# One change to a three-block decoder kernel on one core: the order in which late halves are consumed at six block joints, the start, one table load, and the end of a differential attention

## The reference

```
h    = rms_norm(x, g)                       # mean of squares over the row, then a power of -0.5
y    = swiglu(h, w_in, w_out)               # feed-forward: keys f00, f01, f10, f11 (and f3)
x    = x + rms_norm(y, g2) * factor
gate = sigmoid(x_normed @ w_ple_gate)       # keys p0, p1: one projection times one gate
...
# differential attention (key df), 8 heads, two score maps per head
D    = softmax(q1 k1) - lambda * softmax(q2 k2)
o    = rms_norm(D @ v) per head;  x = x + rms_norm(o @ diff_w_out)
```

## Time and profile before

| | |
|---|---|
| median of three runs | 2924.79 us |
| profiled execution | 2925.86 us |
| its span, first to last instruction | 2924.1 us |
| PE busy | 2855.8 us, 98% |
| DVE busy | 1951.1 us, 67% |
| ACT busy | 1633.9 us, 56% |
| mean granted clock of PE | 0.993 |

### The profile page before, as it was taken

How to read it: one execution, slowest core, us unless ns; L and a number is a source line. 1 busy time by engine, 2 the same in 40 slices (tenths; PEclk the granted TensorE clock), 3 DMA queues, 4 the chain that set the end, 5 groups by cost and what they waited for, 6 DMA issues and landing times.

```text
span 2924.1 us, 44449 instructions
## 1 busy us (share of the span) xinstructions
PE 2855.8 (98%) x17894; PEld 2554.0 (87%) x17894; DVE 1951.1 (67%) x3360; ACT 1633.9 (56%) x2792; POOL 341.2 (12%) x309
## 2 busy tenths in 40 slices
PE   7999999899989999999999999999999999999999
PEld 6878888788878877799998999999888889989997
DVE  5656765676566656758874898777555566656775
ACT  5544654665546555456655444777545455655664
POOL 0000000000010001000000444896000000000000
PEclk9999999999999999999999999999999999999999
DMA  6644556356434554445445554434555564536454
GB/s 205 198 165 145 174 193 224 118 185 217 162 113 144 201 194 147 144 127 169 122 145 187 177 184 159 144 131 145 198 191 193 195 234 133 161 87 208 146 185 154
DMA packets 304525, 490.33 MB, mean 168 GB/s; under 512 B 10865, under 2 KB 236529, under 8 KB 295617
## 3 DMA queue, kind: packets, MB, share of 16 engines
q1 hardware_dynamic: 303184, 480.09, 49.6%
q0 software_dynamic: 1136, 7.41, 0.7%
HBM read 485.36 MB, written 2.10 MB: 167 GB/s over the span
## 4 chain that ended last, share of the span: by engine, by line
PE 88%; DVE 6%; ACT 3%; DMA 1%; issue 1%; POOL 0%; SPq 0%; DVEq 0%; POOLq 0%; ACTq 0%
PE ps L608 30%; PE ps L538 11%; PE ps L542 11%; PE ps L539 10%; PE ps L687 10%; PE ps L686 5%; PE ps L1123 2%; DVE halves L1367 2%; PE ps L559 1%; DVE XX L1405 1%; PE ps L1158 1%; ACT XX L2588 1%; ACT AR L2611 1%; PE ps L1178 1%; PE ps L491 1%
## 5 line engine op out<-in xcount | busy, mean ns | idle before, releaser
L2563 ACT ACTIVATE halves<-raw 128x1024 fp32r<-128x1024 f32 (+1 forms) x842 | 878.4, 1052 | 704.3 <-PE ps L608 336.3
L1367 DVE TENSOR_TENSOR halves<-raw,halves 128x1024 fp32r<-128x1024 f32 (+1 forms) x806 | 965.2, 1219 | 224.3 <-ACT halves L2563 221.6
L538 PE MATMUL ps<-XX,halves 128*128 128x256 f32 (+1 forms) x2360 | 586.4, 286 | 0.0
L539 PE MATMUL ps<-XX,halves 128*128 128x256 f32 (+1 forms) x2360 | 578.2, 283 | 0.0
L608 PE MATMUL ps<-halves,XX 128*128 128x512 f32 x2256 | 527.3, 394 | 5.4 <-DVE XX L1405 2.7
L608 PEld LDWEIGHTS ps<-halves,XX 128*128 128x128 f32 x2256 | 425.9, 190 | 100.9 <-issue 7.9
L538 PEld LDWEIGHTS ps<-XX,halves 128*128 128x128 f32 (+1 forms) x2360 | 451.4, 191 | 2.6 <-issue 2.0
L539 PEld LDWEIGHTS ps<-XX,halves 128*128 128x128 f32 (+1 forms) x2360 | 451.9, 191 | 0.2
L542 PE MATMUL ps<-XX,halves 128*128 128x256 f32 (+1 forms) x2360 | 331.5, 283 | 0.7 <-DVE halves L1367 0.7
L608 PE MATMUL ps<-halves,R 128*128 128x512 f32 x1404 | 322.1, 390 | 0.0
L687 PE MATMUL ps<-XX,halves 128*128 128x512 f32 x1264 | 318.5, 393 | 2.2 <-DVE XX L1405 2.2
(11 more groups left out here) (368 smaller groups left out, 3518.4 us busy)
## 6 DMA issues: line engine op xcount, KB each, us to landing
raw<-in_w_ffn_in SPq DMA_DIRECT2D x88, 1024.0 KB, 5.1
raw<-in_w_in SPq DMA_DIRECT2D x74, 1024.0 KB, 5.3
raw<-in_uT SPq DMA_DIRECT2D x64, 1024.0 KB, 4.8
raw<-in_peer_v SPq DMA_DIRECT2D x64, 1024.0 KB, 4.9
raw<-in_w_ffn_out SPq DMA_DIRECT2D x44, 1024.0 KB, 4.8
raw<-in_w_up SPq DMA_DIRECT2D x24, 1024.0 KB, 5.7
raw<-in_mlstm_w_in SPq DMA_DIRECT2D x12, 1024.0 KB, 5.4
raw<-in_w_down SPq DMA_DIRECT2D x12, 1024.0 KB, 4.9
```

What stands on the lines that cost most here:

```text
L538: mm(o[:, ts], hi[:, q, 0:M], xh[:, k0 + q, ts], start=first and q == 0, stop=False)
L539: mm(o[:, ts], hi[:, q, 0:M], xl[:, k0 + q, ts], start=False, stop=False)
L1367: te.tensor_tensor(lo, src, hi.bitcast(F32), ALU.subtract).then_inc(k.lo_made, 1)
L2563: act(hi, src, ACT.Copy).then_inc(k.hi_made, 1)
```

## The change

It has five edits.

1. In `four`, the term with the low weights comes second and the term with the low half of x last. In DVE's `residual`, at joints that lead to `four`, the low halves of the next weights come first, then the sum into x of side 1, and `enter(0)` is split: four tiles ahead of `x_moment(1)`, four behind it (after p0, four tiles ahead of the sum and four behind it).
2. The start: x is loaded first, in two transfers, and the constants after it. Squares, moment and power are marked per side.
3. In `both_out`, a sigmoid of one column is issued at the end of f01 and f11, after the first two copies.
4. In ml, `decays` starts two steps (one weight piece) later on all three engines.
5. In df, DVE does mix of head 7 before out_pair(2), and ACT and DVE make no halves by `weights()` at t = 0 to 2 but by hand: up to t = 2 first, then t = 3 and t = 4 (ACT after out_pair(2), DVE after attention(8)); the rest comes after out_pair(6).

```diff
@@ tensor_engine, four
             for q in range(3):
-                if q == 2:
+                if q == 1:
                     for m in range(n, n + 4):
                         pe.wait_ge(*k.lo_of(m))
...
-                    for need in ready(t, j, q == 0):
+                    for need in ready(t, j, q < 2):
...
-                             act[q == 1][:, t, j * 128:(j + 1) * 128],
-                             k.halves[:, 0:4, q // 2, t * 128:(t + 1) * 128], ...
+                             act[q == 2][:, t, j * 128:(j + 1) * 128],
+                             k.halves[:, 0:4, q % 2, t * 128:(t + 1) * 128], ...
@@ mlstm decays: PE and ACT range(4) -> range(6), DVE range(2) -> range(4)
@@ sync_engine
+    for j in range(2):
+        load(k.x[:, j], d["x"].rearrange("b (j p) n -> p (b j) n", p=128)[:, j]).then_inc(*dma[f"x_in{j}"].mark(j))
     load(k.cols[:], d["cpack"])...
     load(k.ident[:], ...); load(k.iota[:], ...); load(k.ar(0, 256), ...)
-    load(k.x, d["x"].rearrange("b (j p) n -> p (b j) n", p=128)).then_inc(*dma["x_in"].mark("x"))
@@ vector_engine, residual
         x_moment(0)
+        tokens_next = key in ("f01", "f11", "p1")
+        if not banks:
+            low_to(k.next_four(key) - 3)
+        x_low(0)
+        if not banks:
+            pre(1)
+            if tokens_next:
+                enter(0)
+            low_to(k.next_four(key))
+        if row:
+            weighted(1, 1)
             weighted(1, 0)
             ...
             variance(1)
         if banks:
-            enter(0)
+            if tokens_next:
+                enter(0)
             low_to(k.next_four(key) if more else -1)
+        if row and not banks and not tokens_next:
+            enter(0, range(4))
         if row:
             summed(1)
         else:
             added(1)
+        if not tokens_next:
+            if banks:
+                enter(0, range(4))
+            else:
+                enter(0, range(4, 8))
         x_moment(1)
+        if banks and not tokens_next:
+            enter(0, range(4, 8))
         x_low(1)
         enter(1)
@@ vector_engine, down
-            weights()
+            if t < hold:
+                v.cur += 1
+            else:
+                weights()
@@ vector_engine, diff
+            if t == 0:
+                low_to(v.cur + 2)
+                out_pair(0)
+                for _ in attention(6):
+                    pass
+                last = attention(8)
+                next(last)
+                out_pair(2)
+                for _ in last:
+                    pass
+                low_to(v.cur + 4)
+            if t == 3:
+                for _ in attention(10):
+                    pass
+                out_pair(4)
+                out_pair(6)
-        down("df", 8, True, 1.0, each=before)
+        down("df", 8, True, 1.0, each=before, hold=3)
@@ scalar_engine, diff (down has hold too)
+            if t == 0:
+                high_to(a.cur + 2)
+                out_pair(0)
+                for _ in attention(6):
+                    pass
+                out_pair(2)
+                high_to(a.cur + 4)
+                for _ in attention(8):
+                    pass
@@ scalar_engine
     def both_out(l, c):
         for j in range(2):
             ple_out(l, c, j)
+        if c == 0:
+            act(k.st[:, 90:91], k.cols[:, 0:1], ACT.Sigmoid)
```

More of the change, by code:

```diff
@@ L139, in later, with nothing @@
     yield from side
-def nothing(_):
+def nothing(*_):
     pass
@@ L745, in decays @@
         def decays():
-            for _ in range(4):
+            for _ in range(6):
                 yield
@@ L1282, in normed @@
             gp.wait_ge(*s["xn_high"].need((prev, j)))
-    inverse_root(st[:, 28:30], st[:, 26:28], s["x_var"].need("in"), "in")
+    for j in range(2):
+        inverse_root(st[:, 28 + j:29 + j], st[:, 26 + j:27 + j], s["x_var"].need(("in", j)), ("in", j))
     residual("f00", True, True)
@@ L1397, in turned_x, with of @@
         hi, lo = dst
-        def of(j):
+        def of(j, tiles=range(8)):
             ts = slice(j * 128, (j + 1) * 128)
-            for c in range(8):
+            for c in tiles:
                 c0 = c - c % per
@@ L1521, in tokens, with down @@
                 evac(s0, j)
-    def down(key, KT, row, factor, more=True, each=None):
+    def down(key, KT, row, factor, more=True, each=None, hold=0):
         for t in range(KT):
@@ L1645, in decays @@
             yield from gates()
-            for _ in range(2):
+            for _ in range(4):
                 yield
@@ L2499, in vector_engine @@
     te.tensor_copy(k.mask[:, 0:128], mst[:, 128:256]).then_inc(*step.mark("constants"))
-    v.wait_ge(*s["x_square"].need("in"))
-    chained(te.tensor_reduce(st[:, 26:28], st[:, 16:20].rearrange("p (j h) -> p j h", h=2), AX.X, ALU.add))
-    te.tensor_scalar(st[:, 26:28], st[:, 26:28], 1.0 / 1024, 1e-6, ALU.mult, ALU.add) \
-        .then_inc(*s["x_var"].mark("in"))
-    v.wait_ge(*s["pow"].need("in"))
-    for j in range(2):
+    for j in range(2):
+        v.wait_ge(*s["x_square"].need(("in", j)))
+        chained(te.tensor_tensor(st[:, 26 + j:27 + j], st[:, 16 + 2 * j:17 + 2 * j], st[:, 17 + 2 * j:18 + 2 * j], ALU.add))
+        te.tensor_scalar(st[:, 26 + j:27 + j], st[:, 26 + j:27 + j], 1.0 / 1024, 1e-6, ALU.mult, ALU.add) \
+            .then_inc(*s["x_var"].mark(("in", j)))
+    for j in range(2):
+        v.wait_ge(*s["pow"].need(("in", j)))
         te.tensor_scalar(XN[:, j, 512:1024], x[:, j, 512:1024], st[:, 28 + j:29 + j], None, ALU.mult) \
@@ L2672, in tokens, with down @@
                 evac(s0, j)
-    def down(key, KT, row, factor, more=True, each=None, mid=nothing):
+    def down(key, KT, row, factor, more=True, each=None, mid=nothing, hold=0):
         for t in range(KT):
@@ L2677, in down @@
                 each(t)
-            weights()
+            if t < hold:
+                a.cur += 1
+            else:
+                weights()
         residual(key, lambda j, h: ps[:, aux.of((key, "o", 2 * j + h)), :], True, row, factor, more,
@@ L2927, in before @@
         def before(t):
-            for i in {0: (6, 8), 3: (10,)}.get(t, ()):
-                if i < 10:
-                    out_pair(i - 6)
-                for _ in attention(i):
-                    pass
-                if i == 10:
-                    out_pair(4)
-                    out_pair(6)
-        down("df", 8, True, 1.0, each=before)
+            if t == 0:
+                high_to(a.cur + 2)
+                out_pair(0)
+                for _ in attention(6):
+                    pass
+                out_pair(2)
+                high_to(a.cur + 4)
+                for _ in attention(8):
+                    pass
+            if t == 3:
+                for _ in attention(10):
+                    pass
+                out_pair(4)
+                out_pair(6)
+        down("df", 8, True, 1.0, each=before, hold=3)
     def attend(key, src, E_, yT, release):
@@ L3322, in ffn3 @@
         down("f3", 24, True, 1.0, more=False)
-    a.wait_ge(*k.dma["x_in"].need("x"))
     for j in range(2):
+        a.wait_ge(*k.dma[f"x_in{j}"].need(j))
         for h in range(2):
```

23 lines of the change are left out of this document (4 added, 19 removed).

## The result

| | before | after |
|---|---|---|
| median | 2925.63 us | 2910.24 us |
| its runs | 2924.44 to 2928.08 | 2905.11 to 2911.18 |
| span of the profiled execution | 2924.1 us | 2908.7 us |
| PE busy | 2855.8 us | 2856.3 us |
| mean granted clock | 0.993 | 0.994 |

The ratio is 0.9944, with an interval of 0.9928 to 0.9959: 15.4 us less, where 19.6 were predicted. The four launches of the kernel after lie 6 us apart, and the fastest of them has the highest mean granted clock (0.996; the others 0.993 to 0.995). So the forecast of 2905.2 us is inside what this kernel does, and the spread between launches has to be explained as well as the gain.

A forecast was written before the change was run, and what follows sets the result against it. TensorE, busy 98% of the span, was taken as the bound, leaving 68.3 us to win in, plus half-clock stretches. Terms 4.7 + 3.2 + 0.8 + 5.3 + 1.8 + 3.8 = 19.6 us off 2924.8 gave 2905.2 us, range 2898 to 2914.

The forecast's parts named there:

- Plain joints: Six joints after f00, ml, df, m2, pr, m3: side 1's transposes stop waiting; gain 4.7 us, between 3.5 and 4.7.
- p0: Joint p0 to f10: moved table load, DVE's order and granted clock together gain 3.2 us, between 0.8 and 4.5.
- The three waits foretold: At p0: 0.9 us for a weight's low half, 1.2 for low tiles of x, 1.3 ahead of side 1's transposes.
- The gate's table: Before p0 and p1: the 1.28 us table load moves into ACT's idle time; the chain gains 0.8 us at each.
- Columns: In ml: the 2.8 us wait for gate rows and 2.5 us of low clock go; gain 5.3 us, between 2.6 and 5.4.
- Start: At the start: x first brings the first transpose to about 11.0 us from 12.75; gain 1.8 us, between 0.9 and 2.7.
- End of df: End of df: the wait moves to ACT's late high halves, products start earlier; gain 3.8 us, between 1.5 and 7.
- p1: At p1: the same table load moves, joint order stays; gain 0.8 us, between -0.6 and 2.2.
- a drop of the clock at one place often comes back at another: Rival, whole kernel: clock and df return nothing beyond plain waits; gain only 12.1 us, 2912.7 us; chance 0.2.

The follow-up runs named there:

- the second execution of the change: The whole change measured once more, with no edit against the kernel after: 2906.32 us, ratio 0.9932 to the kernel before.
- edit 4 alone: Only `decays` in ml one weight piece later, against the kernel before: 2922.61 us, ratio 0.9986.
- edit 1 alone: Only the hunks of `four` and `residual` (order of terms and DVE's order at joints), against the kernel before: 2920.39 us, ratio 0.9979.
- edit 5 alone: Only the reordered end of df on DVE and ACT, against the kernel before: 2921.65 us, ratio 0.9983.
- edit 3 alone: Only the sigmoid at the end of f01 and f11, against the kernel before: 2925.44 us, ratio 1.0.
- edit 2 alone: Only x loaded first in two transfers with marks per side, against the kernel before: 2924.93 us, ratio 0.9991.
- halves in the gaps: Late halves of df made in ACT's and DVE's idle time ahead of out_pair(2), on the changed kernel: 2902.3 us, ratio 0.9923 to before.
- old terms: DVE's new order at joints with PE's old order of terms in `four`, against the kernel before: 2924.85 us, ratio 0.9997.
- best: Not defined in the text; the lowest median is the changed kernel with x's moments first and df's late halves in idle time: 2901.8 us.
- early high halves: ACT makes all late high halves of df right after attention(8), on the changed kernel: 2907.39 us, ratio 0.9932 to the kernel before.

## Why the prediction was right, and where its terms were off

- **Plain joints, 4.7 predicted, 5.5 to 6.1 found.** The mechanism holds at each: the wait of 0.7 to 0.8 us goes, nothing is late next. Single joints gave 0.76 to 1.35 us, a little over their waits. I had capped the gain at the wait. What gives the rest was not separated.
- **p0, 3.2 predicted, 4.6 and 3.5 found.** The three waits foretold (0.9, 1.2 and 1.3) came as 0.83, 0.86 and 1.01. They bring side 1's transposes forward by 2.5 us (2.1 predicted; the first of them had stood there before, 0.73 us long). The clock, of which I counted 1.1 of 2.5 us, stayed up in the transposes and in the matmuls behind them, but not always: of the seven profiled executions that have the whole change, five have no half clock at this joint and two, the second execution of the change among them, have 3.4 us of it. The weighing by a half was too low for the first execution and near for these.
- **The gate's table.** By the Trainium skill (ScalarE: Activation LUTs, What ACT_TABLE_LOAD costs), which counts a drain of 1.38 us beside the load, the first side would have been late. The trace does not agree here: ACT's copies end at 506.96, the load follows at 506.97 for 1.28 us, the sigmoid 0.01 us behind it, and 0.56 us of idle time are left over. The prediction gave as a reason that ACT had no work in flight. The rows do not show that: before, too, the load at 536.08 stands 0.02 us behind ACT's copies.
- **Columns, 5.3 predicted, 5.3 found.** The wait and the clock both came back, and edit 4 alone confirms both in its trace. That the number fits so well is in part luck: four of the five other executions without edit 4 have only half as long a low stretch there, and against them the gain would be about 1.25 us less. The 4.2 us by the runs lie near that.
- **Start, 1.8 predicted, 2.3 at the first transpose, 2.7 at the stage's end.** The constants were there at 7.24 and not at 7.5, and the first transpose at 10.48 and not 11.0. The stage's end has a clock term too: before is at half clock from 19.6 to 23.0 us, after is not.
- **End of df, 3.8 predicted, 4.2 found.** The wait changed owner as worked out, to three high halves on ACT, 3.85 us long.
- **p1, 0.8 predicted, 2.1 found**, inside its bounds of -0.6 to 2.2, but by two parts. 1.2 us came at p1 also with edit 1, edit 4 and edit 5 alone, which leave its table load in place: before is at half clock from 1118.7 to 1122.1, and these are not. The other 0.9 us are the table load. Before, no wait stood ahead of side 0's transposes at p1, because PE had been slowed by half clock from 1091.4 to 1094.8. With edit 4 alone PE is not slowed and waits 0.95 us there; with the whole change it is not slowed and does not wait:

```profile
1103.88 1.09 PE L491 MATMUL ps<-ident,AR 128*128 128x128 f32 x8 [0.95 <-ACT AR L2619]
```

```profile
1091.33 1.09 PE L491 MATMUL ps<-ident,AR 128*128 128x128 f32 x8
...
1104.40 1.09 PE L491 MATMUL ps<-ident,AR 128*128 128x128 f32 x8 [0.58 <-ACT AR L2642]
```

The last row is side 1's. After, the stretch from 1095.0 to 1101.8 us is at half clock; side 1's chain on ACT and DVE goes on meanwhile, so part of that loss is caught by its wait (0.58 us where before had 1.87).

**What the sum lacked.** The waits were right in sum. Taken apart, the sum has 16.0 us of waits (4.7 joints, 2.1 p0, 0.8 p1, 2.8 ml, 1.8 start, 3.8 df) and 3.6 us of clock (2.5 in ml, 1.1 at p0). PE's idle time fell by 15.9 us; its busy time, where the clock shows, did not fall by 3.6 but rose by 0.5. So the step that was wrong is the balance of the clock. I priced it where a wait stood ahead of a slow stretch, and took the rest of the kernel as unchanged. By place, the six stretches gave 5.4 us more than the sum has (25.0 against 19.6), much of it clock, and 9.6 us went elsewhere in the first profiled execution, 3.8 in the second. These have opposite signs, and that is why the median of 2910.24 is only 5.0 us off (0.8 of which is the median of before, 2925.63 with its fourth run, against 2924.79). The rival in which "a drop of the clock at one place often comes back at another" had this right in kind, but its price was wrong in place: clock did return behind the waits that went.

**Whether the change makes the drops in df's attention.** Not as a fixed cost: the second execution of the same kernel has none in the longer of the two stretches. Beyond that the two stretches differ. The first, at about 786 to 789 us in before's times, is at half clock for 3.4 or 6.8 us in twelve of the fourteen profiled executions, with edit 3 alone, edit 4 alone and edit 5 alone too; only before and edit 2 alone have none. No single edit is needed for it, and before, profiled once, may just be an exception. The longer one, about 837 to 843 us, is found with edit 1 alone and in four more executions, at the same matmuls, and all five are among the eight that have both halves of edit 1. None of the six others has it. So it may be that edit 1 makes this drop more likely. The runs do not refute that, and eight and six executions are too few to show it.

A low clock comes and goes between launches of one kernel. In each of the thirteen sets of launches the time is the shorter the higher the mean granted clock, with correlations from -0.98 (halves in the gaps) and -0.85 (edit 1 alone) down to -0.17 (old terms). Four sets have -0.36 or weaker (edit 3 alone, edit 5 alone, old terms, the second set of the change), so the mean clock does not carry all of the spread.

**What stays open.** Which of these stretches falls to the low clock in a launch isn't settled. In the first execution after, the record shows no wait of PE in them and only one of 0.16 us a few microseconds ahead (at 821.96; before has the same one and keeps its full clock), and it cannot show very short ones. I saw it in stretches of small matmuls, mostly in df's attention. Each kernel has one profiled execution (the change has two), so "best has three short ones and the first after had two long ones" can be a matter of launches as well as of the kernel. Nor did I separate why the first set of launches of the kernel after (median 2910.24) is 3.9 us above the second (2906.32); they are different sets of four and five launches, with mean clocks of 0.993 to 0.996 and 0.995 to 0.997.

## What to carry to other kernels

Where two engines meet at a joint, move the consumer's order and the producer's order together: DVE's order alone gave 1.3 us, both gave 6.5. When a wait goes, look at what else the same queue releases: the early high halves took away a wait of 3.85 us at the products and brought one of 2.38 us and a low clock one joint later, because the buffers of the next transfer still hung on the low ones. Of a stretch at half clock, price only the one right behind a wait of several microseconds that goes (it came back in all eight executions in ml and in five of seven at p0), and keep some 4 to 10 us of this kernel's 2910 as open for the others. Read a gain against more than one execution of the kernel before: part of what is found at a place can be where that one execution was slow.

## What the runs showed of the hardware

- The granted clock fell to 0.5 in stretches in which the record has PE busy in every microsecond, as in the windows above: 22 matmuls in 6 us at a place where 28 fitted into 5 us at full clock. A busy share of 100% in the record is no promise of a full clock.
- Nor is it proof that PE does not wait: with the old terms the record has PE busy for 6.53 of 6.55 us across two waits of its weight loads for DVE.
- A matmul of 512 columns starts 0.43 us after the last one at half clock and 0.23 us at full clock, a factor of about 1.85. Two windows of before (us, PE, PEld, clock, DMA share, GB/s; L608 alone) show it:

```profile
248.10:251.60 3.50, 3.50 (x8) 2.74 (x9) 0.50 1.07 351
254.70:257.50 2.80, 2.80 (x12) 2.08 (x12) 1.00 0.00 0
```

- The factor of 1.56 that 0.39 against 0.25 us in the prediction gives is too small: the twelve matmuls of 4.69 us end a microsecond after the clock came back at 251.7. A stretch of 3.4 us cost 1.5 us in the attention, where PE had work all through it, and 1.0 to 1.2 us at p1.
